# Rotary row swap of keys and queries: eight permutation products on TensorE replaced by SBUF-to-SBUF transfers issued by ScalarE

## What is computed

```python
def apply_rope(x, cos, sin):
    half = HEAD_DIM // 2                     # HEAD_DIM = 64
    x1, x2 = x[..., :half], x[..., half:]
    return jnp.concatenate([x1 * cos - x2 * sin, x1 * sin + x2 * cos], axis=-1)
...
q_l = apply_rope(project_q(hx, w_qkv), cos, sin)
k_l = apply_rope(k_l, cos, sin)
k_all = jnp.concatenate([k_c, k_l], axis=1)
s = jnp.einsum('bqhmd,bkhmd->bhmqk', q * (HEAD_DIM ** -0.5), k).astype(jnp.float32)
p = jax.nn.softmax(s, axis=-1)
a = p[:, :, 0] - lam * p[:, :, 1]
```

## Time and profile before

| | before |
|---|---|
| time, median of 3 runs | 1120.41 us (1119.83 to 1122.96) |
| span of the profiled execution | 1118.0 us |
| TensorE busy | 1088.7 us, 97% |
| VectorE busy | 825.7 us, 74% |
| ScalarE busy | 546.2 us, 49% |
| bytes moved by DMA | 236.91 MB, mean 212 GB/s |

### The profile page before, as it was taken

The page is one execution under the profiler, slowest core; times in us unless marked ns, Lnnn a source line. Parts: engine busy times, 40 slices in busy tenths (PEclk is TensorE's granted clock), DMA queues, the critical chain, the costliest instruction groups (busy, mean ns, idle before and its releaser), DMA issues.

```text
span 1118.0 us, 15982 instructions
## 1 busy us (share of the span) xinstructions
PE 1088.7 (97%) x6209; PEld 901.7 (81%) x6209; DVE 825.7 (74%) x1285; ACT 546.2 (49%) x842; POOL 114.0 (10%) x99
## 2 busy tenths in 40 slices
PE   4999999999999999999999999999999999999998
PEld 2776777888888888988888898877777788888887
DVE  2678788699999898897764787688674867676753
ACT  1436236464454433545453564757565445545532
POOL 0000000000000015000000002235554000000000
PEclk9999999999999999999999999999999999999999
DMA  9998772767998865876856466534333445666552
GB/s 339 349 322 199 280 264 96 272 226 248 331 314 302 300 247 177 286 253 219 270 193 199 129 210 189 170 97 149 114 113 113 152 153 160 187 186 184 187 196 104
DMA packets 145020, 236.91 MB, mean 212 GB/s; under 512 B 4901, under 2 KB 86322, under 8 KB 144690
## 3 DMA queue, kind: packets, MB, share of 16 engines
q1 hardware_dynamic: 138128, 221.12, 58.9%
q10 hardware_dynamic: 6818, 14.78, 4.2%
HBM read 229.33 MB, written 6.55 MB: 211 GB/s over the span
## 4 chain that ended last, share of the span: by engine, by line
PE 87%; DVE 6%; ACT 2%; POOL 2%; issue 2%; ACTq 1%; DMA 0%; POOLq 0%; DVEq 0%
PE bank L699 83%; PE bank L841 3%; DVE ring_lo L1970 1%; POOL ring_lo L2940 1%; ACTq L1573 1%; ACT w_hi L1539 1%; DMA big<-in_ln_b 0%; POOL x_tok L2983 0%; PE bank L900 0%; POOL x_tok L2976 0%; DVE y_tok L2307 0%; DVE small L2309 0%; DVE small L2781 0%; DVE y_tok L2304 0%; DVE aux L2763 0%
## 5 line engine op out<-in xcount | busy, mean ns | idle before, releaser
L1970 DVE TENSOR_TENSOR ring_lo<-ring,w_hi 128x1024 fp32r<-128x1024 f32 (+4 forms) x290 | 338.0, 1200 | 136.0 <-ACT w_hi L1539 135.6
L1539 ACT ACTIVATE w_hi<-ring 128x1024 fp32r<-128x1024 f32 (+3 forms) x312 | 314.1, 1039 | 244.9 <-PE bank L699 217.3
L699 PE MATMUL bank<-h,w_hi 128*128 128x512 f32 (+1 forms) x1152 | 363.0, 379 | 0.2
L699 PE MATMUL bank<-h,ring_lo 128*128 128x256 f32 x1056 | 281.3, 280 | 0.0
L699 PEld LDWEIGHTS bank<-h,w_hi 128*128 128x128 f32 x1152 | 203.6, 188 | 45.8 <-issue 2.3
L699 PE MATMUL bank<-w_hi,h 128*128 128x512 f32 (+4 forms) x640 | 191.5, 383 | 3.3 <-ACT big L1825 2.2
L699 PEld LDWEIGHTS bank<-h,ring_lo 128*128 128x128 f32 x1056 | 193.1, 189 | 0.5 <-issue 0.5
L699 PEld LDWEIGHTS bank<-w_hi,h 128*128 128x128 f32 x640 | 118.5, 188 | 26.7 <-issue 4.8
L699 PE MATMUL bank<-ring_lo,h 128*128 128x512 f32 (+4 forms) x320 | 115.0, 378 | 0.0
L699 PE MATMUL bank<-w_hi,ff_hi 128*128 128x512 f32 x264 | 103.3, 391 | 0.0
L699 PE MATMUL bank<-w_hi,ff_lo 128*128 128x512 f32 x264 | 102.8, 389 | 0.0
(11 more groups left out here) (276 smaller groups left out, 1341.0 us busy)
## 6 DMA issues: line engine op xcount, KB each, us to landing
aux<-in_w_mod SPq DMA_DIRECT2D x24, 2048.0 KB, 9.6
ring<-in_ffn_w_in SPq DMA_DIRECT2D x88, 512.0 KB, 5.1
ring<-in_w_in SPq DMA_DIRECT2D x24, 1024.0 KB, 5.0
ring<-in_ffn_w_out SPq DMA_DIRECT2D x22, 1024.0 KB, 5.2
ring<-in_w_ffn_in SPq DMA_DIRECT2D x44, 512.0 KB, 4.7
ring<-in_attn_w_qkv SPq DMA_DIRECT2D x12, 1024.0 KB, 12.2
ring<-in_w_ffn_out SPq DMA_DIRECT2D x11, 1024.0 KB, 5.1
bias_rows<-srow ACTq DMA_DIRECT2D x1, 5376.0 KB
```

The source lines that it names most:

```text
L699: return nc.tensor.matmul(o, l, r, start=start, stop=stop, **kw)
L1539: nc.scalar.activation(half_of(i, 0, half), raw_half(i, half), ACT.Copy).then_inc(w_hi, 1)
L1970: V.tensor_tensor(half_of(i, 1, half), raw_half(i, half), half_of(i, 0, half).bitcast(F32), ALU.subtract).then_inc(w_lo, 1)
```

## The change

The permutation matrix, the eight products and their eight PSUM banks are gone. In their place ScalarE issues plain transfers from SBUF to SBUF: for each half `swap_keys(hg)` issues four DMAs, each of 32 partitions x 4 heads x 256 tokens (128 KB), into keys_turned, and for each query pair `swap_queries(pr)` issues four, each of 32 partitions x 2 heads x 256 tokens (64 KB), into queries_turned. That is 24 DMAs and 2 MB in all. The new buffers lie in the space of the buffers prob[0] to prob[3], which the softmax uses only afterwards. VectorE's first pass reads the exchanged rows from SBUF and waits for the DMAs' semaphore, not for a bank.

In ScalarE's program the key transfers of hg 0 stand after `key_copy(3)` and before `query_copy(0)`, those of hg 1 after `key_copy(7)` and before `split_to(10)`; each query transfer stands right behind its `query_copy`.

```diff
-    turned = np.ascontiguousarray(np.concatenate([swap, rope_sin], axis=1).astype(np.float32))
+    turned = np.ascontiguousarray(rope_sin.astype(np.float32))
...
+        keys_turned = v3(aux[:, 9216:9216 + 2 * NB], 4)
+        queries_turned = [v3(aux[:, 9216 + (2 + i) * NB:9216 + (3 + i) * NB], 2) for i in range(2)]
...
-            def swap_keys(pr):
-                for h in (2 * pr, 2 * pr + 1):
-                    wait_emptied(pe, ("K", h))
-                pe.wait_ge(turn_landed, 16)
-                fills(mm(v3(take(("swapK", pr), "misc"), 2), swap, kT[:, 2 * pr:2 * pr + 2, SEQ:], True, True), ("swapK", pr))
...
-                queries(0, 1)
-                swap_keys(0)
-                swap_keys(1)
+                queries(0, 1)
...
-                swap_keys(2)
-                swap_keys(3)
                 queries(1, 1)
...
-                swap_queries(2 * hg)
-                swap_queries(2 * hg + 1)
                 vals(hg, 0, 1)
...
+            def swap_keys(hg):
+                for h in range(4 * hg, 4 * hg + 4):
+                    wait_emptied(act, ("K", h))
+                for b in range(0, P, 32):
+                    act.dma_start(keys_turned[b ^ 32:(b ^ 32) + 32, :, :], kT[b:b + 32, 4 * hg:4 * hg + 4, SEQ:])\
+                        .then_inc(keys_swapped[hg], 16)
+            def swap_queries(pr):
+                wait_emptied(act, ("Q", pr))
+                for b in range(0, P, 32):
+                    act.dma_start(queries_turned[pr % 2][b ^ 32:(b ^ 32) + 32, :, :], qT[b:b + 32, 2 * pr:2 * pr + 2, :])\
+                        .then_inc(queries_swapped[pr], 16)
...
             key_copy(3)
+            swap_keys(0)
             query_copy(0)
+            swap_queries(0)
             query_copy(1)
+            swap_queries(1)
...
             key_copy(7)
+            swap_keys(1)
             split_to(10)
             squares(1)
             query_copy(2)
+            swap_queries(2)
             query_copy(3)
+            swap_queries(3)
...
             def turn_pair(kind, pr):
+                if kind == "K":
+                    buf, turned_rows = kT[:, 2 * pr:2 * pr + 2, SEQ:], keys_turned[:, 2 * (pr % 2):2 * (pr % 2) + 2, :]
+                    dve.wait_ge(keys_swapped[pr // 2], 64)
+                else:
+                    buf, turned_rows = qT[:, 2 * pr:2 * pr + 2, :], queries_turned[pr % 2]
+                    dve.wait_ge(queries_swapped[pr], 64)
...
-                empties(V.tensor_tensor(t, v3(result(dve, ("swap" + kind, pr))[:, :], 2), sin2, ALU.mult), ("swap" + kind, pr))
+                step(V.tensor_tensor(t, turned_rows, sin2, ALU.mult))
```

More of the change, by code:

```diff
@@ L108, in shape_constants @@
     rope_sin = np.concatenate([-sin, sin, -sin, sin], 1).T
-    swap = np.eye(P)[np.arange(P) ^ 32]
     dist = P + np.arange(P)[:, None] - np.arange(SEQ)[None, :]
@@ L270, in build @@
         v_tok = v3(big[:, 6144:10240], 4)
-        swap, rope_sin = big[:, 11776:11904], big[:, 11904:12160]
+        rope_sin = big[:, 11904:12160]
         h_pair = h_both[:].rearrange("p (c m) -> p c m", c=KC)
@@ L340, in build @@
         turn_landed, late_tokens = sem("rope_turn_landed"), sem("late_tokens_low")
+        keys_swapped = [sem(f"keys_swapped{hg}") for hg in range(2)]
+        queries_swapped = [sem(f"queries_swapped{pr}") for pr in range(4)]
         ln_landed, g_landed = sem("ln_landed"), {2: sem("g1_bias_landed"), 5: sem("g2_bias_landed")}
@@ L1062, in vals @@
                     release(key, ins, ("V", hg, tt) if kg == 1 else None)
-            def swap_keys(pr):
-                for h in (2 * pr, 2 * pr + 1):
-                    wait_emptied(pe, ("K", h))
-                pe.wait_ge(turn_landed, 16)
-                fills(mm(v3(take(("swapK", pr), "misc"), 2), swap, kT[:, 2 * pr:2 * pr + 2, SEQ:], True, True), ("swapK", pr))
-            def swap_queries(pr):
-                wait_emptied(pe, ("Q", pr))
-                fills(mm(v3(take(("swapQ", pr), "misc"), 2), swap, qT[:, 2 * pr:2 * pr + 2, :], True, True), ("swapQ", pr))
             def scores(u):
@@ L1574, in _ @@
             act.dma_start(lam_in, a["attn_lambda"][0].partition_broadcast(P)).then_inc(lam_landed, 16)
-            act.dma_start(big[:, 11776:12160], a["const_turn"]).then_inc(turn_landed, 16)
+            act.dma_start(rope_sin, a["const_turn"]).then_inc(turn_landed, 16)
             act.wait_ge(c_landed, 32)
@@ L2162, in turn_pair @@
             def turn_pair(kind, pr):
-                buf = (kT[:, 2 * pr:2 * pr + 2, SEQ:] if kind == "K" else qT[:, 2 * pr:2 * pr + 2, :])
+                if kind == "K":
[4 more added lines that the diff above has]
+                    dve.wait_ge(queries_swapped[pr], 64)
                 t = v3(tmp[:, 0, :], 2)
@@ L2170, in turn_pair @@
                 settle()
-                empties(V.tensor_tensor(t, v3(result(dve, ("swap" + kind, pr))[:, :], 2), sin2, ALU.mult), ("swap" + kind, pr))
+                step(V.tensor_tensor(t, turned_rows, sin2, ALU.mult))
                 step(V.tensor_tensor(buf, buf, cos2, ALU.mult))
-                wait_emptied(dve, ("swap" + kind, pr))
                 settle()
```

## The result

| | before | after |
|---|---|---|
| time, median of 4 runs each | 1120.68 us (1119.83 to 1122.96) | 1130.63 us (1129.04 to 1132.81) |
| ratio, 95% interval | | 1.009 (1.0076 to 1.0105) |
| span of the profiled execution | 1118.0 us | 1127.2 us |
| TensorE busy | 1088.7 us | 1083.9 us |

What follows compares the result with a forecast made beforehand. TensorE was taken to bound the layer up to the first scores, then VectorE's queue. First half +3.3, clock +1.0, second half -0.6 made +3.7: span 1118.0 to 1121.7, plus 2.4 gives 1124.1 us, range 1118.8 to 1128.5.

Steps and rivals of the forecast that it cites:

- What bounds the layer: First half of the attention layer: TensorE up to first values and scores, then VectorE's own queue.
- The products: Eight exchange products leave TensorE at 0.86 us each: a gain of at most 6.9 us, 3.44 in each half.
- The issues on ScalarE, 0.45 each: Four key-transfer issues take ScalarE 1.8 us; hidden in the first half, delaying VectorE's queue in the second.
- The -0.6: Second half of the layer: VectorE's part comes 0.6 us earlier, the issue delay of 1.8 being given back.
- The landing, 76.5: First half: the last key transfer lands at 76.5 us, between bounds 72.1 and 79.2, making the half 3.3 us later.
- From landing to the end of the half: First half: rotation ready 6.4 us after the key landing; everything behind shifts by the landing time minus 73.2.
- L: Time at which the first half's key transfers have landed, taken as 76.5 us; the half is even at 73.2.
- The clock: TensorE's 6.1 us stop before the first half's scores lowers its clock, costing 1.0 us more.
- The query transfers: Both halves: query landings hidden, by only 2 us in the first; in the second landing 161.1, wanted 162.1.
- B: Rival: same key landing, but TensorE's clock holds at 2.4 GHz; +2.7 us, 1123.1 us; chance 0.26.
- C: Rival: transfers don't suffer from load traffic; kernel at 1118.7 to 1119.8 us, not slower; chance 0.16.
- E: Rival: heavy traffic, keys landing at 79.2, query transfers late in the second half; 1127 to 1130.6 us; chance 0.14.

Runs made afterwards that it cites:

- SyncE's first version: Changed kernel, but SyncE issues both halves' exchanges ahead of its loads, bias store behind panel 11's high part: 1121.07 us, 1.0006 of the kernel before.
- the first try with the store: Changed kernel with SyncE's loads held back until the second query exchange landed, bias store placed behind panel 5's high part: 1135.95 us, 1.0128 of the kernel before.

## Why the prediction was wrong, step by step

- **What bounds the layer.** Right. The hand-over points that the forecast reads from VectorE's and ScalarE's queues are those that moved.
- **The products.** Right within the noise: ceiling 6.9, measured 7.5 (5.9 to 9.9) without any exchange, 6.5 in its trace. TensorE's busy time fell by 4.8 us and not by 7: the products are gone (16 instructions fewer), but the first scores and what follows them ran at half clock.
- **The issues on ScalarE, 0.45 each.** Too small. They took 0.61 to 0.75 in after, and 0.95 to 1.04 for the key transfers of three of the other kernels. The price came from one load at the start of the kernel; a transfer of 32 partitions inside SBUF was taken as the same thing. In the first half this put the last key issue at 69.85, which in before's time (1.3 us more) is 71.2 and not 70.1. In the second half it is most of the miss: four issues of 2.70 made VectorE wait 3.0 longer where 1.8 was counted, and 2.1 of it came back until the first query turn (170.42; 162.10 moved by the 7.35 of the first half is 169.45), where the forecast had all of it back. The -0.6 became +0.6 to +1.4 in after and +0.9 in the kernel with that half alone.
- **The landing, 76.5.** This is the failed step. VectorE began at 79.80; with the 1.3 us that after was ahead this is 81.1, or 4.6 us late. It lies 1.9 beyond the upper bound of 79.2 as well. I had drawn a line through two loads (5.8 us plus 0.53 for each 100 KB) and so counted only a fixed time and a rate, from rows of the start of the kernel. What the runs show in its place is a wait for what was issued before on the other queue: 4.3 us behind SyncE's load of 2 MB, and then 7.6 us beside the panels at 94 GB/s. With the loads held back the same transfers landed in 2.5 to 3.8 us each. A row that hints at this stood in the same list, in the kernel before, and I did not read it for this:

```profile
ring<-in_attn_w_qkv SPq DMA_DIRECT2D x12, 1024.0 KB, 12.2
```

A panel of 1 MB, 2.6 us at the 409 GB/s of the earlier trace rows, lands 12.2 us after its issue (panel 6 of the kernel before 12.4, behind the 2 MB issued just ahead of it). So most of its time is not its own. It was the nearest row for a transfer put into this stretch: 68.3 + 12.2 would have been 80.5, and 81.1 came. That the two agree so well is partly luck, since the row is of another queue and of another size.
- **From landing to the end of the half.** Right. The rotation was ready 6.1 to 6.2 after the turn began (6.4 counted with the semaphore); with L = 81.1 the rule "shift = L - 73.2, plus 1.0 for the clock" gives +8.9, and the trace has 96.49 + 1.3 - 89.14 = +8.65.
- **The clock.** Right in kind: it fell during the stop and cost 1.2 us (1.0 counted). The size is partly luck. The stop was 10.4 us and not 6.1, and the price of 1.7 was taken from a row that is not the fall behind the idle start: in the kernel before the stretches 14 to 24 read 1.00, the fall comes behind 25 us, and after, idle as long (to 14.68), has 1.00 from 24 to 30. That TensorE was slow right behind the idle start is seen in its products instead: 32 that take 3.64 us at 42.89 took 6.11 at 17.16, so the reading of 1.00 there seems not to be whole. The row that the prediction took (kernel before):

```profile
24.00:26.00 2.00, 2.00 (x17) 2.00 (x18) 0.28 (x3) 0.00 (x0) 0.00 (x0) 0.90 1.06 390
26.00:28.00 2.00, 2.00 (x11) 2.00 (x11) 1.56 (x4) 0.98 (x3) 0.00 (x0) 0.50 1.06 389
```
- **The query transfers.** Hidden in the first half, as said. In the second the last of them was late by 0.56.
- **The rivals.** B, that a stop of some 6 us leaves the clock alone, is answered by the kernels with the loads held back: behind stops of only 3.35 and 3.40 us the scores ran slower there too (2.86 and 3.79 where 1.99 is usual). C, that the load traffic does not matter, is wrong: only without that traffic does the first turn come at 72.78, L = 74.1 in before's time, near the 73.8 at which C decides. The Trainium skill, "DMA: Bandwidth & Descriptors", section "Anatomy of one DMA", gives 2.0 us plus the bytes at 436 GB/s, an estimate of 2.3 us for 128 KB; the page measured it for DMAs that GpSimd issues, and the prediction used it for ScalarE's. With the loads held back and the store moved away, the four key transfers took 2.4 to 3.6 us (median 2.6), so the traces agree with it nearly where nothing else runs; in after they took 6.8 to 10.6. E had the right reason, heavy traffic, and was given 0.14; its own landing of 79.2 was still too early. That its upper end, 1130.6, is the measured time is luck: it is reached by query transfers that are 3.2 us late in the second half, and these were late by 0.56. With the row of 12.2 as the nearest one this case would have been the likeliest.

The sum: on the span +3.7 was forecast and 9.2 came, which is -1.3 (start) + 8.7 (first half) + 0.9 (second, as in the kernel with that half alone) + 0.9 (at 758 us). Of the miss of 5.5 the first half is 4.4 (8.7 against 4.3, by the landing) and the second half 1.5; the two differences of the executions outside the layer, -1.3 and +0.9, nearly cancel.

## What to carry to other kernels

In this kernel a short DMA on the critical path did not cost its size; it cost what was issued in front of it, on either queue. Before putting one there, read from the trace how long a load of the same stretch takes from issue to landing, list what SyncE and ScalarE have issued in the microseconds before, and issue the short one ahead of the next load or hold the next large store until it has landed: here the same bytes gave +0.9% behind the loads, and -0.4% when SyncE issued them ahead of the loads and the store was held until they had landed.

A saved product on the busiest engine is worth its full length only while no other engine's queue becomes the last one. SyncE's first version lost nearly all of its gain to one wait of 5.5 us.

## What the runs showed of the hardware that was not expected

- A queue's first packets waited for what the other queue had in front. Key packets on ScalarE's queue began only when a 2 MB load ended that SyncE had issued 3 us before them; a fourth transfer waited out a panel of 1 MB issued within a microsecond of it; loads issued 1.4 to 1.8 us behind a 5.4 MB store ran at 2 to 13 large packets a microsecond beside 110 of the store for 7 us, and the panel among them was missing until 19 us after its issue. The Trainium skill, "DMA: Bandwidth & Descriptors", section "Issuing engines are not separate DMA queues", says that DMAs of all engines interleave on the same 16 DMA engines. The trace of after agrees once both queues run (88 to 95 key packets beside 97 to 125 of the panels in a microsecond), but not for the first 4 us. Whether the line is in the DMA engines or in what feeds them, the traces don't tell, and it was not tried.
- Issuing a transfer of 32 partitions inside SBUF took ScalarE 0.61 to 0.75 us in after, and a load of 192 KB 0.45. In three other kernels the first half's key transfers took 0.95 to 1.04 each, in a fourth with the loads held back 0.68; what makes the difference was not tried.
- In the kernel with the loads held back a 2 KB packet inside SBUF took 130 ns on average, a 2 KB packet of a panel load 84 ns, and a packet of keys (1 KB) 70 ns. With no loads beside them the keys moved at up to 190 GB/s, half of what loads reach in the earlier trace rows.
- ScalarE's queue issues a DMA ahead of arithmetic that stands before it in the program if nothing ties them: in the first try with the store, it was issued at 78.05, though the two instructions in front of it began at 78.00 and 78.96. To order it behind them, a wait was needed, not a place.
